# Projection steps in 13 groups per block instead of 22 inside the RWKV chunk phase of a hybrid decoder step

## What is computed

```python
def step(St, inp):
    r_t, k_t, v_t, w_t, kk_t, a_t = inp
    sa = jnp.einsum('bhij,bhj->bhi', St, kk_t)
    St = (St * w_t[:, :, None, :] - sa[..., None] * (kk_t * a_t)[:, :, None, :]
          + v_t[..., None] * k_t[:, :, None, :])
    return St, jnp.einsum('bhij,bhj->bhi', St, r_t)
```

## Time and profile before

| | |
|---|---|
| median of the runs | 3482.54 us |
| profiled execution, span from first to last instruction | 3478.6 us |
| PE busy (its weight loads) | 98% (74%) |
| VectorE busy | 58% |
| ScalarE busy | 36% |
| mean granted TensorE clock | 0.997 of full speed |

### The profile page before, as it was taken

One profiled execution on the slowest core, in us unless ns is written; L12 is line 12 of the kernel. 1 busy time (PEld: TensorE's weight loads), 2 busy tenths in 40 slices (PEclk: granted clock), 3 DMA queues, 4 the chain that ended last, 5 costly groups with the idle time before them and its releaser, 6 DMA issues.

```text
span 3478.6 us, 80470 instructions
## 1 busy us (share of the span) xinstructions
PE 3399.5 (98%) x33076; PEld 2589.1 (74%) x33076; DVE 2030.8 (58%) x5212; ACT 1264.2 (36%) x3599; POOL 243.5 (7%) x284
## 2 busy tenths in 40 slices
PE   7999999999999999999999999999999999999998
PEld 6778686877869778686567787869777687776864
DVE  4656565665656556565346566666656565564653
ACT  2333334242343423524433233333423435234343
POOL 4100100000010000000041001000000000000000
PEclk9999999999999999999999999999999999999999
DMA  8654453626336163252366635436173351732512
GB/s 234 206 175 151 158 178 119 204 75 201 130 115 208 52 211 120 106 186 70 111 200 190 206 125 179 157 126 208 52 236 119 124 176 50 244 104 96 192 56 69
DMA packets 281024, 514.82 MB, mean 148 GB/s; under 512 B 30037, under 2 KB 215571, under 8 KB 268115
## 3 DMA queue, kind: packets, MB, share of 16 engines
q1 hardware_dynamic: 258903, 463.96, 40.7%
q0 software_dynamic: 11648, 41.95, 3.5%
q10 hardware_dynamic: 10108, 3.76, 0.4%
HBM read 473.15 MB, written 47.49 MB: 150 GB/s over the span
## 4 chain that ended last, share of the span: by engine, by line
PE 88%; ACT 4%; DVE 3%; issue 2%; DMA 2%; DVEq 1%; POOL 0%; ACTq 0%; POOLq 0%; SPq 0%
PE bank L823 81%; PE bank L827 7%; DMA win<-in_w_in 1%; DVEq L1555 1%; DMA wout<-in_w_out 1%; ACT Q L2603 1%; ACT PT L2718 1%; ACT qr L2602 0%; DVE mix L1785 0%; ACT Sm L2673 0%; ACT Q L2601 0%; DVE swaa L1783 0%; DVE mix L1781 0%; ACT hT L2426 0%; ACT PT L2523 0%
## 5 line engine op out<-in xcount | busy, mean ns | idle before, releaser
L823 PE MATMUL bank<-hT,win 128*128 128x256 f32 (+3 forms) x6384 | 1190.7, 339 | 6.5 <-DMA win<-in_w_in 3.3
L823 PEld LDWEIGHTS bank<-hT,win 128*128 128x128 f32 (+1 forms) x6384 | 951.1, 186 | 145.0 <-issue 33.4
L823 PE MATMUL bank<-wout,win 128*128 128x128 f32 x3136 | 379.9, 276 | 0.0
L823 PEld LDWEIGHTS bank<-wout,win 128*128 128x128 f32 x3136 | 364.6, 192 | 1.0
L823 PE MATMUL bank<-kv,Q 96*128 96x512 f32 (+3 forms) x640 | 276.4, 529 | 0.2
L1922 DVE TENSOR_REDUCE ml<-bank 128x1 f32<-128x512 f32 (+3 forms) x320 | 195.2, 610 | 124.5 <-PE bank L823 114.1
L827 PEld LDWEIGHTS bank<-cst,Sm 128*128 128x128 f32 x1344 | 157.5, 140 | 134.9 <-issue 72.0
L2673 ACT ACTIVATE Sm<-bank,ml 128x512 f32<-128x512 f32 (+3 forms) x320 | 199.8, 625 | 76.8 <-DVE ml L1927 70.0
L827 PE MATMUL bank<-cst,Sm 128*128 128x128 f32 x1344 | 210.7, 278 | 11.4 <-ACT PT L2523 5.9
L823 PE MATMUL bank<-wout,mix 128*128 128x512 f32 x480 | 215.1, 598 | 2.8 <-DMA wout<-in_w_out 1.7
L2449 ACT ACTIVATE mix<-bank 128x256 f32<-128x256 f32 x128 | 49.0, 383 | 333.1 <-PE bank L823 333.1
(11 more groups left out here) (527 smaller groups left out, 5955.9 us busy)
## 6 DMA issues: line engine op xcount, KB each, us to landing
win<-wfast SPq DMA_DIRECT2D x98, 1024.0 KB, 6.8
win<-in_w_in SPq DMA_DIRECT2D x78, 1024.0 KB, 5.7
win<-wfast SPq DMA_DIRECT2D x98, 768.0 KB, 6.2
wout<-in_w_out SPq DMA_DIRECT2D x60, 512.0 KB, 7.9
out_xres<-xin SPq DMA_DIRECT2D x16, 1024.0 KB
win<-in_w_in SPq DMA_DIRECT2D x16, 896.0 KB, 4.9
PT<-in_w_out SPq DMA_DIRECT2D x28, 512.0 KB, 4.4
XX<-in_w_out SPq DMA_DIRECT2D x28, 512.0 KB, 4.6
```

The source lines that it names most:

```text
L823: return pe.matmul(out, lhsT, rhs, start=start, stop=stop, skip_group_check=True)
```

## The change

The ten groups of three steps in the levels become five groups of six: the three steps that stood between a level's second products and the next level's first products are issued between first and second products. In each chunk the group between the state terms and the product of `XI` with `X0` goes, and the other two groups grow from two steps to three. The number and the order of the steps stay, and so do all other instructions and waits. The last call, which issued what was left (nothing), becomes an assertion.

```diff
@@ -1117,12 +1117,11 @@
                 for lev in range(5):
                     first_product(lev, 0)
                     first_product(lev, 1)
-                    rest(B, 3)
+                    rest(B, 6)
                     if lev == 4:
                         values_of_chunks()
                     second_product(lev, 0)
                     second_product(lev, 1)
-                    rest(B, 3)
                 for j in range(2):
                     for c in range(2):
                         n = j * 2 + c
@@ -1145,13 +1144,12 @@
                         for p in range(2):
                             for h in range(2):
                                 mm(PP[2][half(h), p * 64:(p + 1) * 64], nats[j][half(c), p, 1, half(h)], nats[j][half(c), p, 0, half(h)], p == 0, False)
-                        rest(B, 2)
                         pe.wait_ge(s_x0r.h, s_x0r.at(ip, n + 1))
                         for p in range(2):
                             for h in range(2):
                                 last = mm(PP[0][half(c ^ h), p * P + 64 * h:p * P + 64 * h + 64], XI[j][half(c), 0, 2 * p + h, :], X0[half(c), p, half(h)])
                         last.then_inc(s_sa.h, 1)
-                        rest(B, 2)
+                        rest(B, 3)
                         pe.wait_ge(s_sar.h, s_sar.at(ip, n + 1))
                         for p in range(2):
                             for h in range(2):
@@ -1163,8 +1161,8 @@
                                 mm(o, nats[j][half(c), p, 0, half(h)], gram[j][half(c), 2 * p + h, 2, :], False, False)
                                 last = mm(o, SA[half(c), p, half(h)], gram[j][half(c), 2 * p + h, 0, :], False, True)
                         last.then_inc(s_y.h, 1)
-                        rest(B, 2)
-                rest(B, 74 - B.steps)
+                        rest(B, 3)
+                assert B.steps == 74
```

## The result

The change makes the kernel slower: 3518.6 us against 3482.4 us, median of four runs each, a ratio of 1.0111 (95% interval 1.0099 to 1.0123; the two medians by themselves give 1.0104). The profiled execution has a span of 3516.4 us, 37.8 us more than before. Whole executions of one kernel differ by up to 10 us here (3475.3 to 3486.0 us in 13 runs of the kernel before), most stretches of a block by a few hundredths of one, so what follows is read block by block.

A forecast was written before the change was run, and what follows sets the result against it. PE, busy 98% of the span, bounds the kernel. Levels +2.05 us and chunks +0.4 to 0.5 make about +2.45 us a block, x 16 = +39; 3517.6 on the profiled span, median 3521 us (range 3507 to 3533).

The forecast's parts named there:

- The level boundary: From second products to next large group: 2.51 us XX update, 0.15 until PE starts, 0.39 to next projection: 3.05 us.
- The restart behind a wait: PE between 64x64 groups, from level 1's row: starts 0.15 us after the update, next projection matmul 0.39 us later.
- bound of it: Limits on the restart's cost: 0.16 us less in four levels (10 us), or 0.15 us more in nine places (22 us).
- The large group: Merged group of six steps in a full level: 2 x 1.50 - 0.20 = 2.80 us.
- VectorE's other work: Convolution and rotary work ahead of the XX update: counted as nothing, with about 0.2 us to spare in level 1.
- Chunk 1: SA is ready at 536.41 whatever PE does; earlier steps become waiting and one more comes behind: +0.44 us.
- Chunk 0: Wait of about 0.2 us for X0 against one saved change of shape: from 5.29 to 5.32 us, +0.03.
- The other wait I had named: PE waits of about 0.2 us for X0 in three chunks of four, where none stood.
- The block's price: Levels +2.05 us and chunks +0.4 to 0.5: about +2.45 us a block, x 16 = +39 us.
- the changes of shape decide: Rival: the nine waits do not open and the 52 us saved come in: 3431 us; chance 5%.
- the two cancel: Rival: level boundary costs only half 0's wait (0.35 us), half 1 hidden; 3479 to 3487 us; chance 5%.
- VectorE's other work makes it worse: Rival: masks, convolution and rotary work delay the updates in levels 1 and 2, +1 us a block: 3537 us; chance 8%.

The follow-up runs named there:

- the kernel with more groups: Kernel before with five more groups a block, one of three steps standing between the halves' first products in every level: 3495.5 us, ratio 1.0044.
- the early signal: Changed kernel with VectorE updating the half of XI that the next first products read first, and signalling after it: 3504.1 us, ratio 1.0066.
- the split version: Changed kernel with PE's second products and VectorE's updates split, wanted half first, and a convolution part moved to level 4: 3474.5 us, ratio 0.9988.
- the better versions: Against the kernel before: one six-step group per chunk, 3469.7 us; also level steps moved, 3456.9 us; split second products with one group per chunk, 3459.8 us.
- the kernel with the group on the other side: Kernel before with each level's six steps behind the second products, none between first and second products, chunks as before: 3576.6 us, ratio 1.0277.

## Why the prediction was right

The forecast was 3521 us, the median is 3518.6. The sum was made against the profiled span: +39 us forecast, +37.8 measured. The mechanism was right step by step; that the total was met so closely is in part luck, as the last point below shows. By its own steps, all in block 2, the start of the large group (or of the chunk) counted from that of level 0:

| | before | forecast | after |
|---|---|---|---|
| level 1 | 5.18 | 5.56 | 5.55 |
| level 2 | 9.44 | 9.81 | 9.79 |
| level 3 | 14.59 | 15.66 | 15.63 |
| level 4 | 19.75 | 21.51 | 21.47 |
| chunk 0 | 24.28 | 26.33 | 26.26 |
| chunk 0 lasts | 5.29 | 5.32 | 5.43 |
| chunk 1 lasts | 5.78 | 6.22 | 6.21 |
| chunk 2 lasts | 5.29 | 5.32 | 5.29 |

- *The level boundary.* 2.51 + 0.15 + 0.39 = 3.05 us was the term that carried the sum, and it came out at 3.05 us. The restart behind a wait, the one cost that the trace before showed in a single row, was the same here. Neither bound of it was needed. The term held because it was added up from start to start; the idle times alone would have given 0.44 us less a level.
- *The large group.* 2.80 forecast, 2.79 measured. One group's price is 0.35 us by the kernel with more groups, 0.36 in the forecast.
- *VectorE's other work.* Counted at nothing, and it was nothing: the update in level 1 started 0.22 us after VectorE's last convolution operation ended, the margin that I had named.
- *Chunk 1.* +0.44 forecast, +0.43 measured; the waits went from 0.41 to 0.83 us. The kernel with the convolution's last part behind SA shows the cause.
- *Chunk 0.* Forecast +0.03, measured +0.14 us. I took X0's copies as starting 0.50 us after the chunk, as before. But VectorE now comes late from the last update of XX (531.67 + 0.28) and does Sd ahead of the copy (532.05), so the copy starts 0.65 us after PE's 531.61. The other wait I had named, for X0 in three chunks of four, is listed in chunk 0 alone. In the others PE starts the product 1.04 to 1.05 us after the chunk, as I worked out, and stands 0.13 to 0.14 us before it (in chunk 1 from 537.56 + 0.40 = 537.96 to 538.09), shorter than any wait that the list shows.
- *The block's price.* The sum took 2.45 us a block (2.05 + 0.4); blocks 2, 4, 10 to 13 show 2.55 to 2.57 us from first products to first products. Sixteen times that would be 41 us. That the whole came to 37.8 us is mostly block 0 and block 7: the distance to the next block's first products changes by -0.1 and +0.3 us there. Block 0's levels lose 1.0 us only, and both blocks get more than 1 us back outside the chunk phase. I had multiplied by 16 all the same. What they get back is mostly the clock. The stretches of block 0 (before, after) and of block 7 (before, after), with the granted clock in the third column from the end:

```profile
209.40:213.00 3.60, 3.60 (x6) 1.41 (x5) 3.50 (x10) 0.00 (x0) 0.00 (x0) 0.53 0.40 164
205.00:220.00 15.00, 14.76 (x54) 7.74 (x53) 9.00 (x26) 0.62 (x4) 2.93 (x1) 1.00 0.75 274
...
1730.00:1780.00 50.00, 42.50 (x230) 24.83 (x231) 21.19 (x56) 18.09 (x53) 11.66 (x25) 0.86 0.35 105
1748.00:1798.00 50.00, 43.00 (x238) 25.43 (x237) 22.93 (x60) 19.00 (x60) 11.16 (x25) 0.90 0.38 117
```

In block 0 of the kernel before PE works through 3.6 us at 0.53; at full clock that is about 1.7 us less (an estimate from this row), and in the changed kernel's trace no such stretch stands there. In block 7 the clock is low for less time too. The low stretch in block 0 stands in three of the ten experiments' traces and is missing in the other seven; it stands with the early signal and is missing in the changed kernel, and both have 13 groups. So nothing here ties it to the number of groups, and it was luck that 41 us became 37.8.

The rivals. That the changes of shape decide did not come, though the gain is real: the split version takes part of it. That the two cancel did not come either: the half 1 of the update brings a wait of its own (0.27 us) behind half 0's (0.32 us). That VectorE's other work makes it worse did not come.

The sign followed from one comparison: 2.51 us of update against 1.54 us of PE work, with nothing between them. The draining of which the Trainium skill speaks (TensorEngine Tiling, Key Properties) is there in this case, at 0.35 us for there and back, but a group also covers something, and that was worth more in the levels, the same in three chunks, and less in the groups that the better versions took away.

## What to carry to other kernels

A filler group between two dependent steps has two prices: what its change of shape costs, and what it hides. Read both before merging, from start to start and not by idle time alone: between two small pieces a wait of 0.3 us took 0.5 us here. Take away groups whose wait costs less than the change of shape, and keep or enlarge those in front of the longest wait. When a merge exposes a wait, look at what the waiting engine needs first, and let the other engine do and signal that part first.

## What was not expected of the hardware

- A wait of 2.1 us of PE inside otherwise dense work was followed by some 3 us at a granted clock of 0.50 in 14 of 16 blocks, which cost 1.6 us more each time; in two blocks the same wait was not. The waits of 0.3 to 0.8 us in the chunk phases of the changed kernel were never followed by a lower clock.
- A wait between two 64x64 pieces cost 0.22 to 0.23 us beside its listed idle time, and one of 0.23 us was not listed at all, since the records before it were still running out.
- The stretches of PE work repeat to 0.01 us from block to block and from kernel to kernel (24.90 or 24.91 us from level 0 to the chunks in 12 of 16 blocks before), so a change of some hundredths of a microsecond in a level can be read from one trace, while whole runs of one kernel differ by up to 10 us. Stretches at the low clock that stand in one trace and not in another are likely a part of that.
- A DMA issue on ACT's queue (`out_krope`) that takes 0.49 to 0.50 us in every block of the kernel before took 0.95 to 1.32 us in five blocks of the kernel with the group on the other side, and 0.64 to 1.29 us in five blocks of the changed kernel. Why is open.
